# Three fused blocks on one core: query product in plain fp32 woven into the retrieval, modulation sums on VectorE, row norms by step

## The reference

```python
def first_block(x, c, ...):
    mod = silu(c) @ w_ada + b_ada          # 6 x 1024 scales, shifts and gates
    h = rms_norm(x, norm1_w) * (1 + scale) + shift
    # q, k, v, conv parts, index scores from h @ w_in; top-k mask; attention;
    # x += gate * (concat @ w_out)
    ...
    x = x + gate2 * peer_ffn(h2, ...)

def peer_ffn(h, peer_wq, peer_subkeys, peer_u, peer_v):
    q = (hb @ peer_wq).reshape(B, Q_BLOCK, PEER_HEADS, 2, PEER_HALF)
    s = jnp.einsum('bqhpd,hpnd->bqhpn', q, peer_subkeys)
    vals, idx = lax.top_k(s, PEER_TOPK)     # 8 heads, 16 experts a head and token
    ...
    u_sel = peer_u[expert]
    a = jax.nn.gelu(jnp.einsum('bqhkd,bqd->bqhk', u_sel, hb))
    v_sel = peer_v[expert]
    return jnp.einsum('bqhk,bqhkd->bqd', g * a, v_sel)
```

## Time and profile before

| | us |
|---|---|
| median of 3 runs | 4040.03 (4035.67 to 4041.31) |
| profiled execution, time | 4024.92 |
| its span | 4022.9 |
| busy PE / DVE / ACT / POOL | 3259.2 / 2388.5 / 1419.9 / 1257.1 |
| DMA moved | 896.43 MB, mean 223 GB/s |

### The profile page before, as it was taken

How to read it: one execution, slowest core, us unless ns; L and a number is a source line. 1 busy time by engine, 2 the same in 40 slices (tenths; PEclk the granted TensorE clock), 3 DMA queues, 4 the chain that set the end, 5 groups by cost and what they waited for, 6 DMA issues and landing times. The chain is left out here.

```text
span 4022.9 us, 35798 instructions
## 1 busy us (share of the span) xinstructions
PE 3259.2 (81%) x12074; PEld 2065.8 (51%) x12074; DVE 2388.5 (59%) x4585; ACT 1419.9 (35%) x2251; POOL 1257.1 (31%) x1107
## 2 busy tenths in 40 slices
PE   8999688677666776667678898899399999578888
PEld 5555573222222222222256686677288888456556
DVE  3665474666666666666527646544489889544444
ACT  2323222112221112111114323233378888533443
POOL 0000046777777777777720000000111221100000
PEclk9999799999999999989979998799699999879888
DMA  6233178999999999999952220022599999611111
GB/s 221 66 112 103 49 244 320 355 365 367 359 361 371 361 361 369 371 362 349 371 194 76 59 73 17 27 76 93 199 338 375 373 368 375 226 42 48 32 32 53
DMA packets 421241, 896.43 MB, mean 223 GB/s; under 512 B 38081, under 2 KB 179137, under 8 KB 420418
## 3 DMA queue, kind: packets, MB, share of 16 engines
q0 software_dynamic: 157984, 549.57, 36.5%
q1 hardware_dynamic: 263074, 344.54, 25.3%
HBM read 891.80 MB, written 27.35 MB: 228 GB/s over the span
## 5 line engine op out<-in xcount | busy, mean ns | idle before, releaser
L263 PE MATMUL peer_acc<-peer_vbuf,peer_diag 128*128 128x512 f32 x2048 | 1026.1, 637 | 402.8 <-issue 181.6
L263 PEld LDWEIGHTS peer_acc<-peer_vbuf,peer_diag 128*128 128x128 f32 x2048 | 377.1, 199 | 1049.0 <-issue 897.3
L452 DVE CUSTOM_DVE_ANT_0 peer_junk<-peer_ubuf,firsts_h 128x1024 f32<-128x1024 f32 x512 | 624.7, 1225 | 452.6 <-DMA peer_ubuf<-in_peer_u,peer_experts 336.7
L220 POOL DMA_INDIRECT peer_ubuf<-in_peer_u,peer_experts x512 | 532.7, 1040 | 699.4 <-DVE peer_experts L423 533.8
L228 POOL DMA_INDIRECT peer_vbuf<-in_peer_v,peer_experts x512 | 581.5, 1136 | 230.2 <-issue 125.7
L329 ACT ACTIVATE peer_diag<-all_consts,peer_weights 128x128 f32<-128x128 f32 x512 | 194.5, 398 | 1014.2 <-PE peer_acc L263 469.4
L2985 DVE TENSOR_TENSOR slotted_low<-slotted_raw,slotted_high 128x2048 fp32r<-128x2048 f32 x192 | 434.2, 2289 | 66.1 <-ACT slotted_high L2934 66.1
L2934 ACT ACTIVATE slotted_high<-slotted_raw 128x2048 fp32r<-128x2048 f32 x192 | 365.6, 1920 | 71.1 <-PE slotted_h L2891 51.3
L2752 POOL MEMSET slotted_xg<- 128x4096 f32 x1 | 3.5, 3512 | 774.5 <-POOLq L60 774.5
L2891 PE MATMUL slotted_h<-slotted_high,slotted_xT_high 128*128 128x512 f32 x512 | 205.1, 401 | 6.2 <-DVE slotted_low L2985 4.1
L2891 PE MATMUL slotted_h<-slotted_high,slotted_xT_low 128*128 128x512 f32 x512 | 201.9, 394 | 0.0
(11 more groups left out here) (736 smaller groups left out, 5928.2 us busy)
## 6 DMA issues: line engine op xcount, KB each, us to landing
slotted_raw<-in_moe_w SPq DMA_DIRECT2D x192, 1024.0 KB, 9.2
mixers_raw<-in_w_in SPq DMA_DIRECT2D x56, 512.0 KB, 3.8
firsts_ada_raw<-in_w_ada SPq DMA_DIRECT2D x64, 256.0 KB
third_raw<-in_w_in SPq DMA_DIRECT2D x30, 512.0 KB, 3.7
firsts_raw<-in_w_in SPq DMA_DIRECT2D x28, 512.0 KB, 4.1
firsts_ada_first<-in_w_ada SPq DMA_DIRECT2D x8, 1024.0 KB
peer_s<-in_peer_wq SPq DMA_DIRECT2D x16, 512.0 KB
peer_ubuf<-in_peer_u,peer_experts POOLq DMA_INDIRECT x512
```

Of the source, the lines that this page charges most:

```text
L220: pool.indirect_dma_start(ubuf[:, n % R, :], None, A["peer_u"], bass.IndirectOffsetOnAxis(ap=experts[:, t, m:m + 1], axis=0))\
L263: mm = nc.tensor.matmul(acc[t % 2][j][:, :], diag[:, n % 4, :], vbuf[:, n % R, j * BANK:(j + 1) * BANK], start=(n == t * E), stop=(n == (t ...
L452: nc.vector.tensor_tensor_reduce(junk[:, n % 2, :], ubuf[:, n % R, :], h2[:, t, :], 1.0, 0.0, ALU.mult, ALU.add, act_in[:, t, m:m + 1]).th ...
```

## The change

1. Retrieval: each of the 16 pieces of the query product becomes 8 plain fp32 matmuls straight from the loaded weights; the ACT and DVE splits go, and `h2T` is one fp32 tensor. Ten pieces (AHEAD) stand ahead of the v rows, the other six are put between v rows of heads 0 to 4, one k step to a row (two in head 4). POOL gathers v rows one head behind the u rows from the second head on, and waits for no piece. SP loads two weight pieces ahead of the sub-keys. ACT's order is written out: diagonals of a head in three parts, with exponentials and query copies between them.
2. First mixer: the 64 chunks are multiplied and summed on DVE, 8 to an accumulator of 128x512, and one matmul with a matrix of ones per 8 chunks sums over partitions. Keys, periods and steps of the plan are new.
3. Mixers: "ab" has the tokens as the moving operand (24 matmuls of 512 columns into 8 partitions), one ACT copy and four turns.
4. Routing and third block: row norms in a written order by step over the tiles, two DVE operations in place of three, POOL's adds of the third block on DVE.

```diff
-    KB, NQ, PIECE_US, HEAD_US = 1024, 2 * PH, 5.5, 24.0
+    KB, NQ, AHEAD = 1024, 2 * PH, 10
+    woven = {0: (10,), 1: (11,), 2: (12,), 3: (13,), 4: (14, 15)}
+    scores_after = {1: 5, 3: 6, 4: 7}
...
+                for m in range(NQ):
+                    if m >= 2:
+                        sp.wait_ge(multiplied, m - 1)
+                    sp.dma_start(w_raw[:, m % 2], A["peer_wq"][:, tile(m)].rearrange("(k p) n -> p k n", p=P))\
+                        .then_inc(w_in[m % 2], 16)
+                    if m == 1:
+                        sp.dma_start(skT[:, :, :], A["subkeys_T"]).then_inc(sk_in, 16)
...
                         if g < G:
                             gather_u(g * PT + i)
-                        if g == 2:
-                            if i == 0:
-                                pool.wait_ge(multiplied, NQ)
-                            gather_v(2 * i)
-                            gather_v(2 * i + 1)
-                        elif g > 2:
+                        if g:
                             gather_v((g - 1) * PT + i)
...
+                def product(m, k):
+                    if k == 0:
+                        pe.wait_ge(w_in[m % 2], 16 * (m // 2 + 1))
+                        if m >= 2:
+                            pe.wait_ge(q_moved, m - 1)
+                    mm = nc.tensor.matmul(acc[1][m % 2][:, :], w_raw[:, m % 2, k, :], h2T[:, k, :], start=(k == 0),
+                                          stop=(k == KD - 1))
+                    if k == KD - 1:
+                        mm.then_inc(multiplied, 1)
...
+                for h in range(PH):
+                    steps = [(m, k) for m in woven.get(h, ()) for k in range(KD)]
+                    per = len(steps) // KD
+                    for i in range(PT):
+                        add_row(h * PT + i)
+                        for step in steps[i * per:(i + 1) * per]:
+                            product(*step)
...
+                for m in range(AHEAD):
+                    query_moved(m)
+                    if m >= 3 and m % 2 == 1:
+                        first_scores(m // 2 - 1)
+                    if m == 4:
+                        exponentials(0)
+                first_scores(AHEAD // 2 - 1)
+                for g in range(1, G + 1):
+                    t, h = divmod(g, PH)
+                    gelu(g - 1)
+                    diagonals(g - 1, 0, PT // 2)
...
-                 + stationary("k", W[:, DA:2 * DA], 4), 6.9),
+                (stationary("v", W[:, 2 * DA:3 * DA], 4), 9.0),
+                (stationary("q", W[:, 0:DA], 4) + stationary("k", W[:, DA:2 * DA], 4), 6.0),
...
-                 + stationary("cb", W[:, 3 * DA:4 * DA], 4), 11.0),
-                (closing, 5.6)]
+                 + stationary("cb", W[:, 3 * DA:4 * DA], 4), 8.0),
+                (closing[0:2], 8.0), (closing[2:], 5.6)]
...
+            return 2.25 * q - 4.0 if q < FIRST else 140.0 + 2.6 * (q - FIRST)
...
-                mm = nc.tensor.matmul(side[j % 2][:, :], c_col[:, k:k + 1].broadcast_to([P, P]), ada_raw[:, q % 2, :],
-                                      start=(k == 0), stop=(k == KD - 1))
-                mm.then_inc(ada_used, 1)
+                nc.tensor.matmul(side[j % 2][:, :], C["ones"], ada_acc(j), start=True, stop=True).then_inc(ada_done, 1)
...
+                        dve.wait_ge(ada2_in[q % 2], 16 * (q // 2 + 1))
+                        if k == 0:
+                            dve.wait_ge(ada_done, j - 1)
+                            if q == FIRST:
+                                dve.wait_ge(rectified, len(rels))
+                            ins = nc.vector.tensor_scalar(ada_acc(j), ada_raw[:, q % 2, :], c_col[:, k:k + 1], None, ALU.mult)
+                        else:
+                            dve.wait_ge(ada_used, q)
+                            ins = nc.vector.scalar_tensor_tensor(ada_acc(j), ada_raw[:, q % 2, :], c_col[:, k:k + 1], ada_acc(j),
+                                                                 ALU.mult, ALU.add)
+                        ins.then_inc(ada_used, 1)
...
-        REL_AT, REL_STEP = done_key("iw", 0) + 3.0, 1.9
-        PICK_AT, PICK_STEP = REL_AT + REL_STEP * len(rels) + 2.0, 3.2
+        REL_AT, REL_STEP = done_key("iw", 0) + 3.0, 1.35
+        PICK_AT, PICK_STEP = REL_AT + REL_STEP * len(rels) + 2.0, 3.6
...
-                at += (3.6, 4.4, 5.0, 5.6)[t]
+                at += (3.2, 3.6, 4.2, 4.6)[t]
...
+                        for k in range(KD):
+                            for r, (a, b) in enumerate(three_products((xh[:, k, :], xl[:, k, :]), (wh[:, k, :], wl[:, k, :]))):
+                                mm = nc.tensor.matmul(bank[0:2 * BH, :], b, a, start=(k == 0 and r == 0),
+                                                      stop=(k == KD - 1 and r == 2))
...
+        order = (("mean", 0), ("mean", 1), ("norm", 0), ("mean", 2), ("norm", 1), ("mean", 3), ("norm", 2), ("low", 0), ("low", 1),
+                 ("norm", 3), ("low", 2), ("low", 3), ("low", 4), ("low", 5), ("low", 6), ("low", 7))
...
-                chain(nc.vector.tensor_scalar(x[:, t, :], x[:, t, :], means[:, t:t + 1], roots[:, t:t + 1], ALU.add, ALU.mult))
-                chain(nc.vector.tensor_tensor(x[:, t, :], x[:, t, :], ob[:, 0, :], ALU.mult))
-                nc.vector.tensor_tensor(x[:, t, :], x[:, t, :], ob[:, 1, :], ALU.add).then_inc(x_ready, 1)
+                chain(nc.vector.scalar_tensor_tensor(x[:, t, :], x[:, t, :], means[:, t:t + 1], ob[:, 0, :], ALU.add, ALU.mult))
+                nc.vector.scalar_tensor_tensor(x[:, t, :], x[:, t, :], roots[:, t:t + 1], ob[:, 1, :], ALU.mult, ALU.add)\
+                  .then_inc(x_ready, 1)
...
     def router_scalar(act):
-        yield -20.0
+        yield 9.5
         act.wait_ge(router_loaded, 32)
...
-                pool.wait_ge(y_in[t], 32)
-                nc.gpsimd.tensor_tensor(ya[:, t, :], ya[:, t, :], yb[:, t, :], ALU.add).then_inc(y_added, 1)
```

405 lines of the change are left out of this document (188 added, 217 removed).

## The result

The changed kernel takes **3938.43 us** in the median of four runs (3932.89 to 3953.77), the kernel before beside it 4037.85 us (4031.35 to 4041.31). The ratio is 0.9762, its 95% interval 0.973 to 0.9794: 99 us or 2.4% faster. The forecast was 3922 us, within 3890 to 3972. The time lies inside; the direction is right, the gain is 19 us smaller than the 118 that I had summed.

What follows compares the result with a forecast made beforehand. No one engine was taken to bound the kernel; each stage has its own limit. Terms -60 - 16 - 12 - 15 - 15 = -118 from 4024.92 give 3906.9, plus 15.1 to the median: 3922 us, range 3890 to 3972.

Steps and rivals of the forecast that it cites:

- First mixer, -60 forecast: First mixer: modulation off TensorE and a new order make the stage 60 us shorter, between 34 and 80.
- (b): First mixer, works of the first three tiles, 230 to 363 us: TensorE is full, removed records give -34 us, lesser end -26.
- (c): First mixer, last tile, 363 to 422 us: removed records lay partly in idle time; two works overlap; -8 us, between 0 and -16.
- Hidden in both: First mixer: VectorE's 64 added sums, 44 us, are hidden both before the picks and among the works.
- (a): First mixer, up to the first softmax work: earlier picks, TensorE sets the pace; -15 us, ends -8 and -25.
- (d), the closing: First mixer, closing: two of eight pieces move ahead into the last tile's waits; -3 us, between 0 and -5.
- Retrieval, -16 forecast: Retrieval: v rows gathered earlier fill the hole in DMA transfers; first gather 1 us later; -16 us, ends -22 and +5.
- the term would have been -9: Retrieval: if VectorE's port use slows GpSimd's descriptors in the first head of v rows, the gain is 9 us, not 16.
- "ab", routing, third block: -12, -15, -15 forecast: Later stages: fewer, wider matmuls in the mixers' first piece save 12 us; earlier row norms save 15 us in each other stage.
- A: Rival, first mixer: chunks arrive late, VectorE waits 0.6 us at each, 38 of the 60 us go; about 3960 us; chance 0.17.
- B: Rival: the retrieval gains nothing, through GpSimd's gathers or TensorE's queue; 3938 us, or 3929; chance 0.10.
- I am wrong if the first mixer ends after 460: Sign of failure: first mixer ending after 460 us, or VectorE waiting for chunks more than 20 us in all.

Runs made afterwards that it cites:

- a_only: The kernel before with only the new query product (plain and woven, h2T as one tensor), second chip: 3873.44 us, ratio 0.9961.
- old_plan: The changed kernel with the old plan's periods, closing and due times in the first mixer, modulation still on VectorE, first chip: 3964.79 us, ratio 0.9826.
- pe_late: The changed kernel with the later 32 modulation chunks back on TensorE as fp32 matmuls, first chip: 3957.54 us, ratio 0.9807.
- no_late: The changed kernel without loads and sums of 28 of the 32 late chunks, modulation incomplete, first chip: 3942.94 us, ratio 0.977.
- knorm: The changed kernel with VectorE's multiplications by the q and k norms moved ahead of the last picks, third chip: 3814.52 us, ratio 0.9787.
- b_only: The kernel before with only the modulation sums on VectorE and the new first-mixer plan, second chip: 3860.58 us, ratio 0.9927.
- fine: The changed kernel with first-mixer weight pieces in quarters instead of halves and first two closing pieces cut by tile, first chip: 3939.78 us, ratio 0.9758.

## Why the prediction was right, and where its sum was off

**First mixer, -60 forecast, -22.6 measured.** The step that failed is in (b): "Works of the first three tiles, 230 to 363: TensorE is full", from which I took all 34 us of its removed records. A full engine at a full clock need not be the only bound. The chain score, maximum, exponential, turn, mix was just behind; I named it in (c), for the last tile alone, and held it to be absent from the three before because TensorE showed no idle time there. It showed none because the modulation products filled it. The runs put numbers to it. Under the old order the whole move is worth nothing (a_only and old_plan both end at 484.5). In the new order 24 us of TensorE's load are worth some 16 us of time (pe_late against no_late), and VectorE's sums in their place cost 8.6, so that 7.7 of 24 are left. "Hidden in both", said of the sums, is the second thing that failed. In (a) the picks started as far ahead as said (17 us), but the softmax works did not follow, since the norm's multiplications stood behind the picks on VectorE; I had counted what TensorE runs and not which of VectorE's steps it waits for between the picks' start and end. knorm shows this term at full size: 216.09 for a forecast near 215. (d), the closing, was too small: -13.1 for -3. From the last score read to the stage's end it is 75.6 and 74.7 us with the old h2 and plan, 66.1 with h2 whole alone (a_only), 66.5 with the new plan alone (b_only), and 62.4 to 63.8 with both. h2 was a part that I had left out, and the two do not add.

**Retrieval, -16 forecast, 2 to 12 measured where it can be compared.** The mechanism held: the hole in the transfers is filled (four stretches of 347 GB/s and more, where 124 and 274 stood). What the sum lacks is a loss further on: 7 us of transfer 300 to 400 us into the stage on chips of 405 GB/s, with longer gathers of v rows and behind the last woven step. While the woven steps ran, little was lost, as forecast; whether the later loss is their after-effect is open. The first gather comes 45.0 us into the stage against 42.8, so 2 us where I had 1. From 529 to 589, with VectorE busy 43.7 of 60 us, the gathers of v rows took 1.17 us each on GpSimd (16 of them, 18.7 us), and the transfers kept their rate. By the rule of the page "SBUF — State Buffer", section "SBUF: two separate sides", in the Trainium skill, on GpSimd writing descriptors, the term would have been -9. The stage's total came out near that, but from 529 to 589 there was no loss. Whether the rule bears on the longer gathers behind is not shown: VectorE was no busier there than in the old retrieval.

**"ab", routing, third block: -12, -15, -15 forecast, -11.3, -16.5, -17.5 measured.** Rows with one duration each, a chain of known steps, and nothing else in the stretch.

**Profile and median.** Carrying a difference of 15 us from one profiled run to the median was worth little: before, its sign was right; the profile after is 15 us on the other side, by the gap at 738 perhaps in part.

**Rivals.** A fell: 13.9 us of waits in all 64 sums, against the 38 that it wanted and my limit of 20. What those ahead of the picks cost was not measured. B, a retrieval that gains nothing, is not what happened, though the single profile looks like it: alone on another chip the part gives 14 us (5 to 25 by its interval), 6 to 7 of them in the first mixer. Its time of 3938 was met to the microsecond by chance. "I am wrong if the first mixer ends after 460": it ended at 468.9, and by my own sign this term was wrong.

**The hit.** That the time still lies in the range is in part luck. The first mixer is 37 us short, and the stages of the two profiles sum to 71 instead of 118. The other two chips say much the same, 81 and 84. The 99 us of the first chip's medians hold 28 us more than its two profiles, one of which lay 13 us below its median and the other 15 us above; no trace shows where the median executions save them.

**Open.** How the room that TensorE lost in the works divides between waits and the lower clock as causes of each other: fine and knorm shorten both at once. What lengthens the gathers 300 to 400 us into the retrieval. What the new order gives with the whole modulation on TensorE. What ends ScalarE's unexplained waits on the first chip, and whether its new order adds to them.

## What to carry to other kernels

When work is taken from an engine that is full, price it against the chain that runs beside it: add up one unit's chain across all engines, and take as gain only the difference between that and the engine's load. Price the engine that takes the work over, too: here VectorE's sums gave back half of what TensorE had won. Then look at which small step of another engine the freed one waits for, and where that step stands in its engine's order; here one constant was worth 12.7 us of its stage, where the removal of 128 matmul records under the old order was worth nothing. Cut long blocks on an in-order engine where a chain passes through it. And measure a stage by its own end when another stage's time varies by more than the edit is worth.
